# MoE gather and scatter as three bfloat16 parts, experts paired p and p+8, one activation table set for Ln and Exp

## The reference

```python
def rmsnorm(x, g):
    xf = x.astype(jnp.float32)
    y = xf * lax.rsqrt(jnp.mean(xf * xf, axis=-1, keepdims=True) + NORM_EPS)
    return (y * g.astype(jnp.float32)).astype(x.dtype)

def hier_moe(h, w_rg, w_re, w1, w3, w2):          # 16 experts, hidden width 512
    ...
    # top-1 group of 4, then top-2 of the 4 experts in that group
    combine = jnp.sum(jax.nn.one_hot(expert, MOE_EXPERTS, dtype=jnp.float32) * weight[..., None], axis=1)
    hid = jax.nn.silu(jnp.einsum('nd,xdf->nxf', xt, w1)) * jnp.einsum('nd,xdf->nxf', xt, w3)
    y = jnp.einsum('nxf,xfd->nd', hid * combine[..., None].astype(hid.dtype), w2)
```

## Time and profile before

| | |
|---|---|
| median of 3 runs | 1649.51 us (1648.47 to 1650.92) |
| the profiled execution's own time | 1655.96 us |
| its span (first to last instruction) | 1654.1 us |
| PE busy | 1506.3 us, 91% |
| DVE, ACT, POOL busy | 334.3, 315.9, 81.1 us |
| mean granted clock of PE | 0.954 |
| HBM read | 548.96 MB |
| L717 / L749 / L702 / L757, busy of PE | 446.5 / 226.7 / 134.6 / 119.1 us |

### The profile page before, as it was taken

One profiled execution on the slowest core, in us unless ns is written; L12 is line 12 of the kernel. 1 busy time (PEld: TensorE's weight loads), 2 busy tenths in 40 slices (PEclk: granted clock), 3 DMA queues, 4 the chain that ended last, 5 costly groups with the idle time before them and its releaser, 6 DMA issues.

```text
span 1654.1 us, 18825 instructions
## 1 busy us (share of the span) xinstructions
PE 1506.3 (91%) x7661; PEld 831.5 (50%) x7666; DVE 334.3 (20%) x839; ACT 315.9 (19%) x552; POOL 81.1 (5%) x89
## 2 busy tenths in 40 slices
PE   7999679799999799987999997979999975999997
PEld 3676337454544556755554453554544433444443
DVE  4333341311110222223111011130111024011102
ACT  2211001311111233123111112331111134111112
POOL 1000320010000100001000001010000011000001
PEclk9999879899999899989999998989999987999998
DMA  9778849299999586296499999465999993599993
GB/s 327 320 305 349 367 191 405 109 360 427 428 429 428 247 327 283 78 399 279 204 398 429 429 427 426 197 249 210 423 430 429 427 427 130 210 424 427 428 428 140
DMA packets 40998, 551.98 MB, mean 334 GB/s; under 512 B 4883, under 2 KB 5558, under 8 KB 7654
## 3 DMA queue, kind: packets, MB, share of 16 engines
q1 hardware_dynamic: 38618, 545.78, 79.0%
q0 software_dynamic: 1568, 4.55, 1.0%
q10 hardware_dynamic: 748, 0.74, 0.1%
HBM read 548.96 MB, written 2.10 MB: 333 GB/s over the span
## 4 chain that ended last, share of the span: by engine, by line
PE 85%; DVE 5%; DMA 3%; issue 3%; ACT 2%; POOL 1%; SPq 0%; POOLq 0%; DVEq 0%
PE bank L717 25%; PE bank L749 14%; PE bank L669 12%; PE bank L702 8%; PE bank L757 6%; PE bank L629 6%; DMA ring<-in_w_ada 3%; PE bank L500 2%; PE bank L514 2%; PE bank L779 1%; PE bank L645 1%; PE bank L946 1%; POOL hT L1713 1%; PE bank L727 1%; PE bank L842 1%
## 5 line engine op out<-in xcount | busy, mean ns | idle before, releaser
L717 PE MATMUL bank<-ring,arena 128*64 128x512 f32 x2048 | 446.5, 594 | 2.7 <-ACT arena L1072 2.7
L717 PEld LDWEIGHTS bank<-ring,arena 128*64 128x64 f32 x2048 | 144.2, 137 | 286.9 <-issue 283.4
L749 PE MATMUL bank<-ring,arena 128*64 128x512 f32 x896 | 198.4, 595 | 2.3 <-DVE arena L1345 2.3
L702 PEld LDWEIGHTS bank<-arena 128*128 128x128 f32 x1024 | 126.1, 201 | 28.1 <-issue 22.7
L702 PE MATMUL bank<-arena 128*128 128x128 f32 x1024 | 134.6, 288 | 1.8 <-DVE arena L1325 1.8
L1342 DVE TENSOR_TENSOR arena<-arena,bank 128x512 f32<-128x512 f32 x32 | 22.0, 687 | 502.4 <-PE bank L717 436.1
L749 PEld LDWEIGHTS bank<-ring,arena 128*64 128x64 f32 x896 | 61.9, 137 | 119.2 <-issue 115.9
L757 PE MATMUL bank<-arena 128*128 128x256 f32 x512 | 119.1, 386 | 0.0
L669 PE MATMUL bank<-hT,ring 128*128 128x256 f32 x512 | 113.8, 384 | 1.7 <-DVE hT L1309 1.7
L757 PEld LDWEIGHTS bank<-arena 128*128 128x128 f32 x512 | 94.6, 190 | 37.5 <-issue 26.0
L629 PE MATMUL bank<-ring,condT 128*32 128x512 f32 x768 | 92.9, 639 | 14.3 <-DMA ring<-in_w_ada 14.3
(11 more groups left out here) (244 smaller groups left out, 1133.9 us busy)
## 6 DMA issues: line engine op xcount, KB each, us to landing
ring<-in_moe_w SPq DMA_DIRECT2D x184, 2048.0 KB, 13.2
ring<-in_w_ada SPq DMA_DIRECT2D x48, 2048.0 KB, 14.9
arena<-in_moe_w SPq DMA_DIRECT2D x8, 2048.0 KB, 22.4
ring<-in_hy_w_in SPq DMA_DIRECT2D x6, 2048.0 KB, 11.0
ring<-in_hy_w_out SPq DMA_DIRECT2D x2, 2048.0 KB, 18.6
ring<-in_gla_w_v SPq DMA_DIRECT2D x2, 2048.0 KB, 7.3
ring<-in_gla_w_g SPq DMA_DIRECT2D x2, 2048.0 KB, 7.4
ring<-in_gla_w_o SPq DMA_DIRECT2D x2, 2048.0 KB, 25.4
```

Source lines behind the costliest of these rows:

```text
L702: last = mm(bank[6 + h][:, (k % 4) * P:(k % 4) * P + P], htok[:, g, k * P:k * P + P], sel[:, g].rearrange("p e n -> p (e n)"), start=g == ...
L717: last = mm(bank[4 + kind][SLOTS * e:SLOTS * e + SLOTS, :], xg[:, k, SLOTS * e:SLOTS * e + SLOTS], piece(moe_slots[i][2 * kind + e], KD, F ...
L749: last = mm(bank[6 + h][SLOTS * e:SLOTS * e + SLOTS, :], hidT[:, f, SLOTS * e:SLOTS * e + SLOTS], w2[e][:, f, h * 512:h * 512 + 512], star ...
```

## The change

The gather and the scatter multiply by 0/1 matrices, so that they move numbers and compute nothing. The change splits each float32 operand into three bfloat16 parts that add up to it exactly (the rounded value, the rounded rest, and what is left), and runs three bfloat16 matmuls where one float32 matmul (two instructions) stood. The combine weight can then no longer ride in selT: selT becomes a 0/1 matrix (`is_gt`), and the weight of each slot, wcol, is a row sum that scales y when yv is made. The parts of htok are made ahead of the pairs by ACT, POOL, ACT and DVE in turn; those of yv by ACT, DVE, ACT and DVE for each pair. The scatter of a pair is moved behind h1 of the next pair; that of pair 7 stays at the end. The pairs are now experts p and p+8. Norms name one table set that holds Ln and Exp. Arena addresses are moved to make room; a few semaphores of DVE alone are replaced by a chain.

```diff
-        htok = ar(0, G, D)
+        htok = [ar16(0, G, D), ar16(1024, G, D), ar16(14336, G, D)]
+        htok_raw = ar(2048, G, D)
...
-            src = expert_dram[kind][bass.ds(first_expert + e, 1)].rearrange("o p n -> p (o n)")
+            src = expert_dram[kind][bass.ds(first_expert + PAIRS * e, 1)].rearrange("o p n -> p (o n)")
...
                 def gather(h):
 
                     for k in range(4 * h, 4 * h + 4):
-                        for g in range(G):
-                            last = mm(bank[6 + h][:, (k % 4) * P:(k % 4) * P + P], htok[:, g, k * P:k * P + P],
-                                      sel[:, g].rearrange("p e n -> p (e n)"), start=g == 0, stop=g == G - 1)
+                        for n in range(3 * G):
+                            last = mm(bank[6 + h][:, (k % 4) * P:(k % 4) * P + P], htok[n % 3][:, n // 3, k * P:k * P + P],
+                                      sel[:, n // 3].rearrange("p e n -> p (e n)"), start=n == 0, stop=n == 3 * G - 1)
                     last.then_inc(s(pre + "gathered"), 1)
+
+                def scatter(n, last_pair):
+
+                    pe.wait_ge(s(pre + "selT_ready"), primed(n + 1))
+                    for m in range(KD):
+                        if m % 4 == 0:
+                            pe.wait_ge(s(pre + "yv_rest"), primed(4 * n + 3 + m // 4))
+                        for part in yv:
+                            last = mm(half(m), part[:, m * P:m * P + P], selT[:], start=False, stop=False,
+                                      skip_group_check=True)
+                        if m in (1, 3, 5) and last_pair:
+                            last.then_inc(s(pre + "summed"), 1)
+                    last.then_inc(s(pre + "scattered"), 1)
...
                         if kind == 1:
+                            if not first:
+                                scatter(n - 1, False)
...
-                pe.wait_ge(s("htok_ready"), 2 * (i + 1))
+                pe.wait_ge(s("htok_last"), 4 * (i + 1))
                 moe_round("", PAIRS * i, i)
...
-            def load_table(fn):
-
-                act_fn(small[:, 4:5], one, fn)
+            def load_log_exp():
+
+                nc.scalar.preload_act_table_set("natural_log_exp_and_others")
...
-                    act.wait_ge(s(pre + "selT_mm"), primed(n + 1))
+                    act.wait_ge(s(pre + "selT_ready"), primed(n + 1))
                     act.wait_ge(s(pre + "scattered"), primed(n))
-                    act_fn(selT[:], bank[5][:, 0:NT], ACT.Copy).then_inc(s(pre + "selT_ready"), 1)
-                    act.wait_ge(s(pre + "y_mm"), primed(n * 2 + 1))
-                    act_fn(yv[:, 0:512], bank[6][:], ACT.Copy).then_inc(s(pre + "yv_lo"), 1)
+                    for h in range(2):
+                        act.wait_ge(s(pre + "y_mm"), primed(n * 2 + h + 1))
+                        act_fn(yv[0][:, 512 * h:512 * h + 512], bank[6 + h][:], ACT.Identity, scale=wcol) \
+                            .then_inc(s(pre + "yv_big"), 1)
+                    for h in range(2):
+                        act.wait_ge(s(pre + "yv_rest"), primed(n * 4 + h + 1))
+                        act_fn(yv[1][:, 512 * h:512 * h + 512], yr[:, 512 * h:512 * h + 512], ACT.Copy) \
+                            .then_inc(s(pre + "yv_big"), 1)
...
                     for h in range(2):
-                        last = act_fn(htok[:, g, h * 512:h * 512 + 512], bank[2 * g + h][:], ACT.Copy)
-                    last.then_inc(s("htok_ready"), 1)
+                        for dst in (htok_raw, htok[0]):
+                            last = act_fn(dst[:, g, h * 512:h * 512 + 512], bank[2 * g + h][:], ACT.Copy)
+                        last.then_inc(s("htok_big"), 1)
 
                     act.wait_ge(s("route_in"), 2 * i + g + 1)
                     act_fn(*route_exp[g], ACT.Exp).then_inc(s("route_exp"), 1)
+                for n in range(4):
+                    act.wait_ge(s("htok_rest"), 4 * i + n + 1)
+                    cols = slice(512 * (n % 2), 512 * (n % 2) + 512)
+                    act_fn(htok[1][:, n // 2, cols], htok_raw[:, n // 2, cols], ACT.Copy).then_inc(s("htok_big"), 1)
...
-                    dve.wait_ge(s(pre + "y_mm"), primed(n * 2 + 2))
+                    dve.wait_ge(s(pre + "selT_mm"), primed(n + 1))
                     dve.wait_ge(s(pre + "scattered"), primed(n))
-                    v.tensor_copy(yv[:, 512:1024], bank[7][:]).then_inc(s(pre + "yv_hi"), 1)
...
+                    v.reduce_sum(wcol, bank[5][:, 0:NT], AX.X)
+                    tt(selT[:], bank[5][:, 0:NT], zero.broadcast_to([P, NT]), ALU.is_gt) \
+                        .then_inc(s(pre + "selT_ready"), 1)
...
+                        stt(yr[:, cols], bank[6 + h][:], wcol, yv[0][:, cols], ALU.mult, ALU.subtract) \
+                            .then_inc(s(pre + "yv_rest"), 1)
...
+                        tt(yv[2][:, cols], yr[:, cols], yv[1][:, cols], ALU.subtract).then_inc(s(pre + "yv_rest"), 1)
...
                 tt(over[0:1, 0:1], r_rd[0:1, 3:4], r_rd[0:1, 2:3], ALU.add).then_inc(s("rounds_known"), 1)
+                for n in range(4):
+                    dve.wait_ge(s("htok_big"), 8 * i + n + 5)
+                    cols = slice(512 * (n % 2), 512 * (n % 2) + 512)
+                    tt(htok[2][:, n // 2, cols], htok_raw[:, n // 2, cols], htok[1][:, n // 2, cols], ALU.subtract) \
+                        .then_inc(s("htok_last"), 1)
...
+            def token_rests(i):
+
+                for n in range(4):
+                    pool.wait_ge(s("htok_big"), 8 * i + n + 1)
+                    cols = slice(512 * (n % 2), 512 * (n % 2) + 512)
+                    v.tensor_tensor(htok_raw[:, n // 2, cols], htok_raw[:, n // 2, cols], htok[0][:, n // 2, cols],
+                                    ALU.subtract).then_inc(s("htok_rest"), 1)
```

More of the change, by code:

```diff
@@ L180, in build @@
         small = sb("small", [P, 5])
-        eps, one, rstd_col = small[:, 0:1], small[:, 1:2], small[:, 2:4]
+        eps, one, rstd_col, zero = small[:, 0:1], small[:, 1:2], small[:, 2:4], small[:, 4:5]
         rw = sb("rw", [P, KD, 20])
@@ L237, in build @@
         hidT = ar(4096, 4, P)
[L238 to L241, removed]
+        yv = [ar16(4608, D), ar16(5120, D), ar16(5888, D)]
+        yr = ar(7040, D)
+        sel = ar16(5632, G, 2, SLOTS)
+        selw = ar(6496, G, 2, SLOTS)
+        selT = ar16(5760, NT)
         comb = ar(6400, G, EXPERTS)
@@ L437, in _ @@
                     slot_free(moe_slots[i][4 + e])
-                    expert_load(sp, 2, e, i, EXPERTS * i + 2, "full")
+                    expert_load(sp, 2, e, i, EXPERTS * i + 1, "full")
                 for kind in range(2):
@@ L442, in _ @@
                     for e in range(2):
-                        expert_load(sp, kind, e, i, EXPERTS * i + 2, "full")
+                        expert_load(sp, kind, e, i, EXPERTS * i + 1, "full")
                 with sp.Fori(2, PAIRS) as p:
@@ L449, in _ @@
                         for e in range(2):
-                            expert_load(sp, kind, e, i, EXPERTS * i + p * 2, "full")
+                            expert_load(sp, kind, e, i, EXPERTS * i + p, "full")
                 rounds = needed_rounds(sp, i)
@@ L736, in pair @@
                     pe.wait_ge(s(pre + "hidT_ready"), primed(n + 1))
-                    if first:
+                    if first and pre == "":
                         w2 = first_w2[i]
@@ L752, in pair @@
                         last.then_inc(s(pre + "y_mm"), 1)
[L753 to L761, removed]
                 for m in range(4):
@@ L768, in moe_round @@
                 gather(1)
-                if pre == "":
-                    pair(0, True, first=True)
-                with pe.Fori(0 if pre else 1, PAIRS - 1) as p:
+                pair(0, True, first=True)
+                with pe.Fori(1, PAIRS - 1) as p:
                     pair(p, True)
                 pair(PAIRS - 1, False)
+                scatter(b + PAIRS - 1, True)
             def moe(i):
@@ L1042, in norm @@
             def norm(n):
-                load_table(ACT.Ln)
+                load_log_exp()
                 for k in range(KD):
@@ L1320, in _, with by_pair @@
             g1 = lambda i: lambda m, g: mod[:, i, 16 + m, g:g + 1]
+            def by_pair(x, p):
+                return x.rearrange("p g (e n) -> p g e n", e=2)[:, :, :, bass.ds(p, 1)].broadcast_to([P, G, 2, SLOTS])
             def build_sel(pre, n, p):
-                r = rank[:, :, bass.ds(p * 2, 2)].unsqueeze(3).broadcast_to([P, G, 2, SLOTS])
+                r = by_pair(rank, p)
                 io = iota.unsqueeze(1).unsqueeze(1).broadcast_to([P, G, 2, SLOTS])
@@ L1493, in _ @@
             v.tensor_copy(upper16[:], upper)
-            v.tensor_copy(mask[:], mask32).then_inc(s("mask_ready"), 1)
+            chain(v.tensor_copy(mask[:], mask32))
             ada_at("start")
```

50 lines of the change are left out of this document (33 added, 17 removed).

## The result

The changed kernel takes **1655.46 us** (median of 15 runs, 1651.85 to 1661.38) against 1649.51 (15 runs beside them, 1647.28 to 1654.11): ratio **1.0036**, 95% interval 1.0027 to 1.0045. It is slower by 5.9 us. The forecast was about 1660 us and slower.

What follows compares the result with a forecast made beforehand. PE was taken to bound the kernel, with DMA a close runner-up. Per MoE +10.9 ahead of the pairs, -7.4 in them, +2.0 at the last scatter, times four, less 11.6 for tables: +10.4 us, about 1660 (range 1640 to 1672).

Steps and rivals of the forecast that it cites:

- term (1): Gather and scatter on PE: a bfloat16 matmul costs 62 ns for 128 columns and 115 ns for 256.
- the rival of 80 ns: Gather's weight loads hardly hidden, 80 ns a step: first gather 1.4 us more per MoE, 1669 us; chance 0.11.
- term (2): Pairs of each MoE: loads become the bound, and y of pair 7 ends 7.4 us sooner behind pair 0.
- the rival "the loads are not the bound": In the pairs PE's sum counts, not the weight loads: -13.2 us per MoE, 1637 us; chance 0.07.
- the rival "the clock falls": PE's clock drops in waits for loads and ahead of the last scatter: up to 3 us per MoE, 1671; chance 0.12.
- term (3): Last scatter of each MoE: waits for yv's parts, DVE starts 3.1 us behind y, +2.0 us.
- term (4): Before pair 0: DVE held, its subtractions, exposed matmuls on zeros and a low-clock gather cost +10.9 us per MoE.
- The hold: Router chain before pair 0: DVE held to the end of each of POOL's four subtractions, 4.1 us late.
- The rival "no hold": Before pair 0 POOL does not hold DVE: 4.1 us per MoE falls away, 1643.5 us, faster; chance 0.25.
- term (5): Norms and attention: nine table loads of 1.283 us between Ln and Exp go away, -11.6 us in all.

## Why the prediction was right, and where its steps were not

The measured time lies in the forecast's range, and the mechanisms were the right ones. But the direction came out right by luck: the term ahead of the pairs holds an error of counting of 12 us, and without it the same working says "no change". The sizes erred in both directions and partly cancelled.

- **Price of the bfloat16 matmuls, term (1)**: right, 60 and 114 ns against 62 and 115. The Trainium skill's 81 ns (TensorE: Matmul & The Clock Gate, Back-to-back issue gap) is not what this stream shows: 24 steps of 128 columns, each with its own weights, take 1.45 us. The measurement decides, and with it the rival of 80 ns is out.
- **The body, term (2)**: -4.4 to -5.7 instead of -7.4 a layer. The mechanism is shown, by the ring waits in after and by the run with short w2; the rival "the loads are not the bound" is out. The gain fell short of the forecast by two things. Y of pair 7, held by the last w2, starts 212.9 to 213.4 us behind the start of h1 of pair 0 instead of 211.7. In layer 2, w1 of pair 2 lands only 4.3 us earlier, against its pair 0 (44.3 us behind it, 48.6 in before), and the 17 pairs of loads behind it take 168.5 us (to 1332.6), not 167.7. And in layers 1 and 2 y of pair 7, which follows a wait, takes 8.79 and 8.80 us where 7.10 stands in the other two. In those two it is h1 of pair 7, behind its own wait, that takes 8.78; that costs 0.5 us at the start of y (213.4 instead of 212.9). This is a part of the rival "the clock falls".
- **The last scatter, term (3)**: +9.1 over four layers, +8.0 forecast. The wait ahead of L723 is 2.25 us in every layer, as summed (2.2). In layers 1 and 2 DVE's additions start 3.11 us behind y, as forecast (3.1). In layers 0 and 3 the 24 steps take 4.45 us (granted clock 0.61 in the window of layer 0 shown below) and DVE starts 3.5 to 3.6 us behind y. Float32 there, which has no such wait, took 11.4 us off the tails.
- **Ahead of the pairs, term (4)**: +25.7 over four layers instead of +43.6. Here a step failed. The first gather was counted as 96 bfloat16 steps (17 at 122 ns and 79 at 62), but the program has 48, as the earlier trace rows show: 32 float32 instructions are 16 float32 matmuls, and three parts of each make 48. With 31 behind the 17 the same working gives 4.0 us, and 3.97 was measured; the count made the term 3.0 us a layer too large, 7.9 being left of the 10.9. Measured in layer 0: +6.6. The hold was there and mis-sized: DVE's chain ends 3.1 us later behind the last router matmul (12.54 us behind its start, 9.42 before), not 4.3. POOL's four operations took 4.48 us, 1.12 each, not 1.27. DVE's four subtractions took 2.48 us, not 2.75. The rival "no hold" is out.
- **The tables, term (5)**: -12.4 measured, -11.6 forecast.

With the right count the sum would have been -1.5 us instead of +10.4, and the forecast "no change" at about 1648. The stages and the tables together give 25.7 - 20.2 + 9.1 - 12.4 = +2.2 us; the medians say +5.9. Nearly 4 us are in no stage of the two profiled executions. The start-up varies by more than that between traces of code that does not differ there (the first group of L669 begins at 57.47 us in before, 55.14 in after, 50.56 with the table set alone), so one execution of each can't place the rest, and it stays open.

## What to carry to other kernels

- Where one operand is a 0/1 matrix, three bfloat16 matmuls in place of one float32 matmul saved about 25% of PE's time on it here (2.73 us against 3.65), but the other operand has to be split by a chain of operations on other engines. Use them where that chain lies under other PE work, and keep float32 where PE would have to wait for the chain: here, at the first gather and the last scatter, worth 35 us of 1655.
- When PE gets faster, first look at how far the weight stream is behind it. Here it had 2.8 us to spare, and it kept back 8.2 of the 13.2 us that PE saved in a layer's pairs, as the run with short w2 shows.
- Where one matmul stands in the trace as two instructions, count the new matmuls from the program: 32 instructions of the float32 gather became 48 bfloat16 steps, not 96.

## What the runs showed of the hardware

- DVE operations on 8 or 32 columns with both operands in SBUF are held until POOL's operation beside them ends (0.63 to 1.10 us against 0.17 and 0.21 alone, POOL's being 1.15 us long). DVE's reductions, with one input, take 0.16 to 0.19 us under the same POOL operations. This is the exclusive lock of the Trainium skill (SBUF — State Buffer, Who interferes with whom); the trace agrees.
- Behind a wait of 2.2 to 2.3 us ahead of a scatter PE's granted clock fell in some places and not in others. In layer 0 of after, 24 steps took 4.45 us at a granted clock of 0.61. In layer 0 of the run with the first gather in float32 the same wait, at the same place, was followed by 24 steps in 2.78 us at 1.00. Over the traces of the eight kernels with this wait, 17 of the 32 last scatters are slow (4.05 to 4.45 us); without it (before, the tables alone, and the two kernels with the last scatter in float32) none of 16 is. In none of the nine layers where y of pair 7 had just been slow (8.8 us) was the scatter behind it slow too. A row with a wait of this length should be priced both ways.

The wait and the scatter in after (us, busy of PE, PEld, DVE, ACT, POOL, then PEclk, DMA share, GB/s):

```profile
541.90:544.20 2.30, 0.07 (x2) 0.01 (x1) 1.38 (x3) 1.83 (x3) 0.00 (x0) 1.00 1.04 442
544.20:548.60 4.40, 4.38 (x24) 3.13 (x24) 3.46 (x12) 2.95 (x5) 1.28 (x2) 0.61 0.99 423
```

The scatter at the same place of the run with the first gather in float32:

```profile
539.90:542.70 2.80, 2.78 (x24) 2.26 (x24) 2.59 (x9) 2.18 (x4) 0.09 (x1) 1.00 1.00 427
```
